# The experts' down product with sample and prompt taking turns over each half of the contraction

## What is computed

```
aff = softmax(x @ w_router)
gsel, idx = top_k(aff per expert, cap)               # cap: 64 sample, 16 prompt
xs  = x[idx]
hdn = silu(xs @ w_gate[e]) * (xs @ w_up[e])          # 1024 -> 1024
out = (hdn @ w_down[e]) * gsel                       # 1024 -> 1024
y   = zeros.at[idx].add(out)
```

## Time and profile before

| | us |
|---|---|
| median of three runs | 2959.09 |
| the profiled execution, its own time | 2958.45 |
| its span | 2956.7 |
| TensorE busy | 2737.6 |
| VectorE busy | 980.2 |
| ScalarE busy | 605.1 |
| GpSimd busy | 156.8 |
| expert stage, first layer | 775.34 to 1317.14 |
| expert stage, second layer | 2371.97 to 2913.59 |

### The profile page before, as it was taken

One profiled execution on the slowest core, in us unless ns is written; L12 is line 12 of the kernel. 1 busy time (PEld: TensorE's weight loads), 2 busy tenths in 40 slices (PEclk: granted clock), 3 DMA queues, 4 the chain that ended last, 5 costly groups with the idle time before them and its releaser, 6 DMA issues.

```text
span 2956.7 us, 43676 instructions
## 1 busy us (share of the span) xinstructions
PE 2737.6 (93%) x18603; PEld 1584.2 (54%) x18603; DVE 980.2 (33%) x2500; ACT 605.1 (20%) x1361; POOL 156.8 (5%) x212
## 2 busy tenths in 40 slices
PE   6999999979699999988899898999998699999994
PEld 1456449965244444431466548999984444444442
DVE  1100106653311111102277616667764511111113
ACT  3110011134000101003266312222224200000003
POOL 0000000000011111110000000000000011111110
PEclk9999998989799999998999999999999699999997
DMA  8511200022799999978411000000002679999994
GB/s 280 198 48 39 78 0 1 1 72 107 274 378 386 391 393 393 387 285 284 142 57 58 29 14 1 1 1 2 1 1 71 245 287 385 390 389 392 391 390 164
DMA packets 184238, 547.68 MB, mean 185 GB/s; under 512 B 15761, under 2 KB 28441, under 8 KB 184105
## 3 DMA queue, kind: packets, MB, share of 16 engines
q1 hardware_dynamic: 170345, 517.39, 46.0%
q0 software_dynamic: 13760, 28.38, 4.2%
HBM read 517.89 MB, written 27.86 MB: 185 GB/s over the span
## 4 chain that ended last, share of the span: by engine, by line
PE 78%; DMA 10%; DVE 6%; ACT 3%; issue 1%; SPq 1%; DVEq 0%; POOL 0%; ACTq 0%
PE ps L1220 13%; PE ps L816 9%; DMA qkv<-in_w_up_dram 8%; PE ps L826 7%; PE ps L1228 6%; PE ps L773 6%; PE ps L1250 5%; PE ps L1152 4%; PE ps L1114 3%; PE ps L1268 3%; PE ps L817 2%; PE ps L1096 2%; PE ps L893 2%; PE ps L1128 1%; PE ps L804 1%; PE ps L963 1%
## 5 line engine op out<-in xcount | busy, mean ns | idle before, releaser
L1220 PE MATMUL ps<-slots,wk 128*64 128x512 f32 x1536 | 360.7, 596 | 3.7 <-DMA qkv<-in_w_up_dram 3.6
L816 PE MATMUL ps<-hT,slots 128*128 128x512 f32 x640 | 334.2, 604 | 3.1 <-ACT hT L474 3.1
L1250 PE MATMUL ps<-qkv,og 128*64 128x512 f32 x1024 | 233.9, 598 | 6.4 <-ACT og L703 3.3
L1220 PEld LDWEIGHTS ps<-slots,wk 128*64 128x64 f32 x1536 | 106.3, 137 | 212.5 <-issue 208.7
L826 PE MATMUL ps<-slots,hT 128*128 128x512 f32 x480 | 209.7, 597 | 0.0
L817 PEld LDWEIGHTS ps<-hT,slots 128*128 128x128 f32 x640 | 123.5, 193 | 156.6 <-issue 156.6
L773 PE MATMUL ps<-slots,cnd 128*2 128x512 f32 x384 | 172.8, 605 | 33.6 <-DVE x L1842 22.6
L1228 PE MATMUL ps<-slots,wk 128*32 128x256 f32 x3072 | 196.6, 381 | 0.0
L1790 DVE COPY idc<-idT 128x1 uint32 (+1 forms) x96 | 11.9, 152 | 514.4 <-DMA moe_p<-og,idc 514.3
L826 PEld LDWEIGHTS ps<-slots,hT 128*128 128x128 f32 x480 | 92.0, 192 | 112.1 <-issue 111.8
L1228 PEld LDWEIGHTS ps<-slots,wk 128*32 128x32 f32 x3072 | 93.4, 110 | 106.8 <-issue 51.9
(11 more groups left out here) (284 smaller groups left out, 3689.7 us busy)
## 6 DMA issues: line engine op xcount, KB each, us to landing
slots<-in_w_gate_dram SPq DMA_DIRECT2D x64, 2048.0 KB, 15.3
qkv<-in_w_down_dram SPq DMA_DIRECT2D x64, 2048.0 KB, 19.0
slots<-in_w_up_dram SPq DMA_DIRECT2D x32, 2048.0 KB, 19.9
qkv<-in_w_up_dram SPq DMA_DIRECT2D x32, 2048.0 KB, 21.8
slots<-in_w_ada_dram SPq DMA_DIRECT2D x24, 2048.0 KB, 8.0
slots<-in_w_in_dram SPq DMA_DIRECT2D x16, 2048.0 KB, 8.1
slots<-in_w_out_dram SPq DMA_DIRECT2D x4, 2048.0 KB, 16.7
xn_d<-og SPq DMA_DIRECT2D x10, 512.0 KB, 2.6
```

The costliest lines, as they stand in the source:

```text
L816: mm(PS[:, b, :], w, hT[:, kt, P:TOK], start=(kt == 0), stop=(kt == KT - 1))
L1220: ins = mm(PS[c * 64:(c + 1) * 64, i, :], xsT[q][:, kt, 0:CAPS], wide[j + i][:, k, c * HC:(c + 1) * HC], start=(kt == 0), stop=(kt == KT - 1))
L1250: ins = mm(PS[c * 64:(c + 1) * 64, 4, :], hdS[:, k * P + hf * 64:k * P + hf * 64 + 64], wide[4 + hf][:, k, c * HC:(c + 1) * HC], start=(ft ...
```

## The change

The two functions of the down product become one. The wait for the prompt's inner rows and their two transposes go ahead of the whole down product. The order of the matmuls becomes sample half 0, prompt half 0, sample half 1, prompt half 1. `hp_in` is awaited ahead of prompt half 0, and `down_s` is raised after sample half 1, with prompt half 1 still to come. `moe_free` count 3 is raised after prompt half 0 and count 4 after prompt half 1. The number of matmuls and transposes is the same.

```diff
-                def down_sample(e, first):
-
+                def down(e, first):
+
+                    pe.wait_ge(S("hid_p"), L * PER["hid_p"] + e + 1)
+                    if not first:
+                        pe.wait_ge(S("op_ready"), L * PER["op_ready"] + e)
+                    for k in range(2):
+                        t2 = tr(PS[:, 5, 256 + k * P:256 + (k + 1) * P], ebP[:, k * P:(k + 1) * P], ident)
+                    t2.then_inc(S("hp_turned"), 1)
                     pe.wait_ge(S("hs_in"), L * PER["hs_in"] + e + 1)
                     if not first:
                         pe.wait_ge(S("os_ready"), L * PER["os_ready"] + e)
...
                         if hf == 0:
-                            pe.wait_ge(S("hid_p"), L * PER["hid_p"] + e + 1)
-                            if not first:
-                                pe.wait_ge(S("op_ready"), L * PER["op_ready"] + e)
-                            for k in range(2):
-                                t2 = tr(PS[:, 5, 256 + k * P:256 + (k + 1) * P], ebP[:, k * P:(k + 1) * P], ident)
-                            t2.then_inc(S("hp_turned"), 1)
-                    ins.then_inc(S("down_s"), 1)
-
-                def down_prompt(e):
-
-                    pe.wait_ge(S("hp_in"), L * PER["hp_in"] + e + 1)
-                    for hf in range(2):
+                            pe.wait_ge(S("hp_in"), L * PER["hp_in"] + e + 1)
+                        else:
+                            ins.then_inc(S("down_s"), 1)
                         for k in range(4):
                             ft = 4 * hf + k
                             for c in range(4):
...
-                    down_sample(e, first)
-                    down_prompt(e)
+                    down(e, first)
```

## The result

The changed kernel takes **2966.26 us** in the median of 12 runs (2959.23 to 2968.55), the kernel before 2959.36 (2956.39 to 2963.03, 12 runs). The ratio is 1.002, with a 95% interval from 1.0011 to 1.0029: 0.1 to 0.3% slower, on both sides of the 0.2% that the prediction took as its bound. Of the kernels further down, after_again and before_late each had one execution in a slower state of the chip; their ratios leave it out, their medians don't. The profiled execution took 2966.62 us with a span of 2964.8.

What follows compares the result with a forecast made beforehand. Bound: TensorE (33.69 us per expert) and the weights' stream (33.99), nearly equal. At +0.32 us per expert, layers +2.4 and +3.7 make +6.1; with scatters +0.8, 2958.45 + 6.9 = 2965.3 us, range 2959.5 to 2971.5.

Steps and rivals of the forecast that it cites:

- Who sets the end: Expert stages: the weights' stream hides 2.76 and 1.44 us of TensorE's time; at 34.01 us per expert TensorE sets the end.
- The product, -0.23: Down product on TensorE: in the new order it takes 10.90 us per expert instead of 11.13, 0.23 less.
- The wait, +0.55: Ahead of the down product: waiting for VectorE's prompt rows, then two transposes, starts sample half 0 0.55 us later per expert.
- The first layer, +2.4: First layer's expert stage: 16 x 0.32 less the 2.76 us hidden by the stream, +2.4 us.
- The second layer, +3.7: Second layer's expert stage: 16 x 0.32 less 1.44 us hidden, +3.7 us, if the register operations stay.
- The scatters, +0.8, up to 1.5: End of each layer's stage: the prompt's scatter issued 0.40 us later, +0.8 in all, up to 1.5 if both slow each other.
- The stream's gap and the earlier load: Weights' stream: w_down half 0 loads earlier, worth 0.4 us once per layer, only if the stream still set the end.
- The stream as the end (1): Expert stages: the stream goes on setting the end, not slower, 2958.5 us at least, some 2960; chance 0.26.
- sequencer work in every expert (2): Behind the new wait on TensorE: register operations in every expert, slower by more, 2969 to 2975 us; chance 0.17.
- the third: Down product: transposes find rows ready, TensorE saves 0.23 and 0.13 us per expert, the change pays, about 2958 us; chance 0.05.

Runs made afterwards that it cites:

- after_again: The changed kernel, unaltered, run once more as a second set of runs for a second trace: 2964.81 us, ratio to the kernel before 1.001.
- before_late: The kernel before with one more VectorE operation (a multiplication by 1) ahead of the last one on the prompt's rows: 2958.58 us, ratio to the kernel before 0.999.

## Why the prediction was right

The forecast was 2965.3 us and the median is 2966.3. The mechanism was right: TensorE sets the end, a wait and two transposes stand uncovered ahead of a product that gets 0.23 shorter. That the number came within 1 us is partly luck: the parts that can be read sum to 5.2 us, where 6.9 had been forecast, and the median moved by 6.9 (interval 3.3 to 8.6), the second set of runs by 4.7.

- **Who sets the end.** Right, and confirmed by taking the load away: the stream had hidden 2.88 and 1.59 us (541.80 - 538.92, 541.62 - 540.03), against 2.76 and 1.44 worked out. TensorE was expected to overtake the stream with experts of 34.01 us. It did so with 33.97, although that lies just below the stream's 33.99: over 16 experts its own 543.4 us exceed the 541.8 of the stream, which starts with a lead.
- **The product, -0.23.** Measured 10.90, to the hundredth: sample halves 3.59, prompt halves 1.86.
- **The wait, +0.55.** Measured +0.51. The copy and VectorE end as assumed (864.70 and 864.83, 0.13 apart), the transposes take 0.36, and the release was 0.06 where 0.10 had been taken. The lower bound of 0.05 was nearly the right value: the semaphore instruction that had been given another 0.05 doesn't show. So +0.28 per expert, not +0.32, 1.3 us less over 32 experts.
- **The first layer, +2.4.** Measured +1.6: 16 x 0.04 = 0.6 by the wait, and the stream had hidden 0.1 more than worked out.
- **The second layer, +3.7.** Measured +2.2. Besides the same 0.6 and 0.15 more hidden, the term mis-sized is that the register operations stay as dear. There are still 6, but an expert that has one takes 34.04 instead of 33.97, 0.07 more and no longer the 0.19 that the working took from the earlier trace rows. In the trace the operation now stands between VectorE's end (2468.21) and the transposes (2468.34), a release of 0.13. That makes 6 x 0.12 = 0.7 us.
- **The scatters, +0.8, up to 1.5.** Measured +1.44, the upper end. The later issue was +0.27 instead of +0.40, but the landing got 0.41 to 0.47 longer, which the working had only named as a possibility.
- **The stream's gap and the earlier load.** No effect, as said, since TensorE sets the end. The reason given, that an earlier place in the queue moves nothing while the DMA engines are busy, isn't shown by this; freeing the gate slot sooner did shorten the stages.
- **Rivals.** The stream as the end (1) and sequencer work in every expert (2) can be ruled out by the two stages; the third would have needed the transposes to find their rows ready, and the trace shows them waiting in all 32 experts.

## What to carry to other kernels

Work that waits for the end of another engine's chain is free only as long as other work of its own queue stands ahead of it: moved ahead of the product, the two transposes put off its start by 0.51 us, and a further 0.32 us on VectorE then went straight into every expert's time. Count what leaves the old place too: here the product got 0.52 us shorter, the transposes and one change of shape, so that the move alone cost nothing. Taking turns between two shapes then cost two changes of shape, 0.29 us. Count those changes first, and what stays behind the result that someone waits for at the end of the stage. When a stream and an engine are within 1% of each other, take load off the stream once: it shows how much of the engine's time is hidden, to some tenths of a us. What the change was meant to give the stream, a slot freed sooner, could be had by an order of matmuls that costs TensorE nothing.

## What the runs showed of the hardware

- A change between the sample's and the prompt's tile shape costs 0.13 us behind the prompt's matmuls and about 0.16 behind the sample's, and short blocks are no dearer than long ones. The prompt's: 3.59 - 2 x 1.73 for 64 matmuls and 1.86 - 1.73 for 32. The sample's: two of its matmuls start every 0.429 us (weight loads of line 1220 from 877.06 to 882.21, twelve steps, in the trace of after), so 16 take 3.43 of their 3.59 us and 32 take 6.87 of their 7.02.

```profile
877.06 0.14 PEld L1220 LDWEIGHTS ps<-slots,wk 128*64 128x64 f32 x2 [0.29 <-issue]
...
882.21 0.14 PEld L1220 LDWEIGHTS ps<-slots,wk 128*64 128x64 f32 x2 [0.29 <-issue]
```

- A register operation behind a wait costs 0.19 us ahead of the product's first weight load (six experts of before) but 0.07 ahead of the transposes (six experts of after). The first waits for ScalarE's copy and the second for VectorE's last operation; why they differ wasn't tested.
- An indirect DMA that adds rows to DRAM landed later where another was issued shortly before it: in 4.08 us when it went 1.86 us after the other (after), in 3.67 when it went 3.31 us after it (before).
- The mixers' times wander by some us between runs (the stage's start by 9.4 over eleven traces). Expert stages that TensorE sets repeat to 0.03 us, those that the stream of weights sets differ by 0.5 to 0.8.
